# Three joint units at each norm: x times scale first, inverse root and shift on their PSUM banks

## Chip, core and metric

The kernel runs on one core of one Trainium2 chip. The metric is the device time of one execution in microseconds; the time before is the median of three runs. PE is TensorE, DVE is VectorE, ACT is ScalarE, POOL is GpSimd, SP is the queue that issues the weight loads.

## What is computed

A trunk of two layers over 128 context tokens and 256 latent tokens, D = 1024, all in fp32. What matters here is where the norms stand:

```
h   = rmsnorm(x) * (1 + scale1) + shift1
u, q, k, v, z, xbc, dt = split(h @ w_in)            # three mixers, gates, merge
x   = x + gate1 * (merged @ w_out)
h2  = rmsnorm(x) * (1 + scale2) + shift2
up  = dwconv3(h2 @ ffn_w_up)
x   = x + gate2 * ((silu(up_a) * up_b) @ ffn_w_down)
```

`rmsnorm` divides each token by the root of its mean square over D (plus 1e-6). Scale, shift and gate are vectors of D for each of the two token groups, the six parts of `silu(c) @ w_mod + b_mod`.

## The kernel before

Activations lie transposed: 128 channels on the partitions, eight tiles of channels, and 386 columns for the tokens: 256 latent ones, a gap of two columns (`LAT:CTX0`), 128 context ones. The gap is zero; the three-tap convolutions read across it. Every product is made of three matmuls (`three`, lines 787 to 789): a value is cut into a high half that TensorE takes without loss and a low half, and high x high, low x high, high x low are summed in one PSUM bank. ScalarE makes the high halves (line 1102 for weights, 1119 for activations), VectorE the low ones (1423 and 1428).

The work of a layer is a list of units, one weight tile of 128x1024 each: 8 XBC, 4 UU, 4 QQ, 4 KK, 4 VV, 4 ZZ, 24 GATE, 12 BRANCH, 8 OUT, 44 UP, 24 DOWN (three for each of 8 output tiles). Every engine walks that list in order in a program of its own and waits on semaphores of the others; so an instruction that waits holds all behind it on its engine. Four PSUM banks are used in turn by the groups, and a unit may open its bank when the group four before has been read (`group_read`). Three weight tiles are held as halves, four as raw data: when unit u is done, ScalarE makes the high half of unit u+3 and VectorE the low half (`ahead`, lines 1121 and 1430), which TensorE waits for (`wait_lo`).

After a unit of XBC or UP, ScalarE evacuates the bank with the centre tap (`evac`, 1199), VectorE adds the outer taps (`taps`, 1549 and 1551), ScalarE makes a tanh (1237) and VectorE a product (1558, 1562 or 1568); a pair of UP groups then gives a tile `ah`, `al` for DOWN.

An OUT or DOWN group is added into x by VectorE (`update`, 1606, two pieces, latent and context), ScalarE squares the tile (1181) and GpSimd sums the squares (605). At a norm TensorE multiplies that sum by a matrix of ones (`mean_squares`, 739), ScalarE makes the inverse root `rs` (1112, 1113), and then tile by tile VectorE makes x times rs (1443), ScalarE scale and shift (1141, two pieces) and the high half (1119), VectorE the low half (1428). The three first units behind a norm are joint: for each tile of h their three products are made together, so that they follow the norm tile by tile (`joint`, 852). There are four norms with joint units: N1 and N2 of layers 0 and 1, and a last one without units.

The scale, shift and gate vectors are made by VectorE as well, from streamed tiles of `w_mod`: one tile after a unit given by `mod_places` (126), two multiply-and-sum passes of 128x1024 (`modulation`, line 1477), against rows of silu(c). Layer 0 has such tiles after 16 units UU to VV, after 8 units in the mixers, after every third UP unit from UP2 on (14), and after the first 22 DOWN units; layer 1 after the 12 units before ZZ and after every fifth UP unit from UP4 on (8). The rows are loaded anew for the FFN and turned into silu by ScalarE (`row_tanh`, 1171) and VectorE (`rows_silu`, 1463) right behind the second norm.

Of the kernel before, what the change touches and what calls it, by code (L numbers as in the profile page):

```python
# [30 lines left out]
P = 128  # L31
# [52 lines left out]
DOWN0 = U_OF[(DOWN, 0, 0)]  # L84
PREP = DOWN0 + MOD_HEAD + 2
MIX0 = U_OF[(ZZ, 0, 0)]
UU0, BRANCH0, OUT0 = U_OF[(UU, 0, 0)], U_OF[(BRANCH, 0, 0)], U_OF[(OUT, 0, 0)]
# [38 lines left out]
def mod_places():  # L126

    tiles = [(l, m) for l in range(DEPTH) for m in range(MODT)][MOD_HEAD:]
# [78 lines left out]
def scan_task(s, lag=0):  # L207

    y_, rest = divmod(s - lag - SLOT_Y, Y_SLOTS)
    return y_ if rest == 0 and 0 <= y_ < NY else None  # L210


# [59 lines left out]
def build(nc, wstream, whead, par, bias, tab, xs, xp, cvec, cvec_rows, kc, vc, st0, fng, y, newk, newv, news):  # L272
    ctx = ExitStack()
    with ctx:
# [99 lines left out]
        fg = sb("fg", [P, KT])  # L374
        bm = sb("bm", [P, NBIAS])

        acc_all = ctx.enter_context(nc.psum_tensor("acc", [P, BANKS, 512], F32))
# [60 lines left out]
        sq_sum = sem("sq_sum")  # L438
        rs_ready = sem("rs_ready")
        h_full = sem("h_full")  # L440
        h_hi = sem("h_hi")
# [291 lines left out]
        def _(pe):  # L733
# [57 lines left out]
            def unit(l, u):  # L791
# [47 lines left out]
                else:  # L839
                    g = G_OF[(kind, j)]  # L840
                    bank = open_bank(g)
                    first = SP_MG if (kind, j) == (OUT, 0) else None
                    srch, srcl = (mh, ml) if kind == OUT else (hh, hl)
# [7 lines left out]

            def joint(l, u0, split0):

                kind = UNITS[u0][0]
                banks = []
                if l == 0 and u0 == 0:
                    pe.wait_ge(crow_ready, 2)
                for i in range(JOINT):
                    wait_lo(pe, l * NU + u0 + i)
                    g = G_OF[(kind, i)]  # L860
                    if g >= BANKS:
                        group_read(pe, l, g - BANKS)
                    banks.append(acc[g % BANKS])

                def product(i, k):
                    s = (l * NU + u0 + i) % NHL
                    return three(banks[i][:, 0:T], wh[:, s, P * k:P * k + P], wl[:, s, P * k:P * k + P], hh[:, k, :],
                                 hl[:, k, :], k == 0, k == KT - 1)

                for k in range(KT - 2):  # L870
                    if l == 0 and u0 == 0 and k in (2, 4):
                        shift_pair(k // 2 + 1)
                        shift_sums(k // 2 + 1)

                    pe.wait_ge(h_lo, count(l, NSPLIT, split0 + k))
                    for i in range(JOINT):
                        product(i, k)
                pe.wait_ge(h_lo, count(l, NSPLIT, split0 + KT - 1))
                for i in range(JOINT):
                    product(i, KT - 2)  # L880
                    product(i, KT - 1).then_inc(unit_used, 1)

# [189 lines left out]
            for l in range(DEPTH):  # L1072
                if l:
                    mean_squares(l, 0, 2 * l)
                for u in range(NU):
                    if u in (0, UP0):
                        if u:
                            mean_squares(l, M_N2, 2 * l + 1)
                        joint(l, u, SP_N2 if u else SP_N1)
# [10 lines left out]
        def _(act):  # L1090
# [35 lines left out]

            def norm(l, nth, split0, scale, shift0):

                for j in range(KT):
                    b = cv[:, j % 2, :]  # L1130

                    act.wait_ge(h_full, count(l, NFULL, (F_N2 if nth else F_N1) + j))

                    if l == 0 and nth == 0:
                        if j % 2 == 0 and 2 <= j <= KT - 4:
                            shift_part(j // 2 + 1)
                        act.wait_ge(scale_ready, j // 2 + 1)
                    else:
                        act.wait_ge(scale_ready, KT // 2 + 2 * l + nth)
                    for v, (a0, a1) in enumerate(SEGS):  # L1140
                        last = af(b[:, a0:a1], b[:, a0:a1], ACT.Identity, bias=mod[:, shift0 + j, v:v + 1],  # L1141
                                  scale=scale[:, j, v:v + 1])
                    step.then(last)
                    high(l, None, hh[:, j, :], b)

# [37 lines left out]
            def evac(l, g):  # L1183
                kind, j = GROUPS[g]
                bank = acc[g % BANKS]
                group_done(act, l, g)
                if kind in (XBC, UP):
                    n = j if kind == XBC else 8 + j
# [159 lines left out]
            for l in range(DEPTH):  # L1348
# [7 lines left out]
                norm(l, 0, SP_N1, sc1, 0)  # L1356
                if l == 0:
                    params(l)

                act.wait_ge(par_ready, l + 1)  # L1360
                for u in range(NU):
                    if u == UP0:
                        inv_rms(l, M_N2, D)
                        norm(l, 1, SP_N2, sc2, 3 * KT)
# [6 lines left out]
                    if u in (0, UP0):  # L1371
                        ahead(l, u)
# [6 lines left out]
                    for g in done:  # L1379
                        kind, j = GROUPS[g]  # L1380
                        if kind in (XBC, UP):
                            conv_silu(l, g)
                            if kind == UP and j % 2:
                                high(l, F_FF + j // 2, ah[:, j // 2, :], cv[:, 1, :])
                        if kind in (OUT, DOWN):
                            first = KT * (2 * l + (kind == DOWN))
                            square(first, j, first + j)
                        if kind == BRANCH and j >= 2 * KT:
                            high(l, F_MG + j - 2 * KT, mh[:, j - 2 * KT, :], cv[:, j % 2, :])
# [23 lines left out]
        def _(dve):  # L1413
# [21 lines left out]

            def norm(l, nth, split0):

                dve.wait_ge(rs_ready, 2 * l + nth + 1)
                for j in range(KT):
                    if j >= 2:  # L1440

                        dve.wait_ge(h_lo, count(l, NSPLIT, split0 + j - 2))
                    tt(cv[:, j % 2, :], x[:, j, :], rs[:, :], ALU.mult).then_inc(h_full, 1)
                    if j:
                        low(l, split0 + j - 1, hl[:, j - 1, :], cv[:, (j - 1) % 2, :], hh[:, j - 1, :])
                low(l, split0 + KT - 1, hl[:, KT - 1, :], cv[:, (KT - 1) % 2, :], hh[:, KT - 1, :])

# [320 lines left out]

            low_merged = []

            dve.wait_ge(cs_in, 32)
# [5 lines left out]
            for l in range(DEPTH):  # L1777
# [19 lines left out]
                else:  # L1797
                    norm(l, 0, SP_N1)
                for u in range(NU):
                    if u == UP0:  # L1800
                        norm(l, 1, SP_N2)
                        rows_silu(l + 2, crow, junk_ffn)
                    if u == PREP and l + 1 < DEPTH:
                        params(l + 1)

                        summed(l + 1, 0, MOD_HEAD)
                        scale_of(sc1, norm1_weight(l + 1), KT).then_inc(scale_ready, 1)
                    if u in (0, UP0):
                        ahead(l, u)
                    done = done_after(u)  # L1810
                    for g in done:
                        if GROUPS[g][0] in (XBC, UP):
                            group_done(dve, l, g)
                            taps(l, g)
                        if GROUPS[g][0] == BRANCH:
                            branch(l, g)
# [5 lines left out]
                    for g in done:  # L1822
# [11 lines left out]
                        if kind in (OUT, DOWN):  # L1834
                            update(l, g)
                    while low_merged:
                        jj = low_merged.pop(0)
# [3 lines left out]
                    if last_update:  # L1841
                        ahead(l, u)
                    if (l, u) == (0, LATE_ROWS):
                        rows_silu(1, crow_late, junk_late)
                    modulation(l, u)
                    if u == MIX0 - 1:

# [137 lines left out]
```

## Time and profile before

| what | value |
|---|---|
| median of 3 runs | 1437.79 us (1434.54 to 1438.02) |
| the profiled execution | 1435.48 us, span 1433.7 us |
| PE busy | 1349.9 us, 94% |
| DVE busy | 1058.4 us, 74% |
| ACT busy | 651.9 us, 45% |
| POOL busy | 155.8 us, 11% |
| mean granted TensorE clock | 0.974 of full speed |
| last chain, by engine | PE 64%, DVE 22%, issue 6%, ACT 6% |

The busy shares are averages over stages. In 650 to 710 us, in the DOWN stage of layer 0, VectorE is busy over 99% while TensorE is too; in the second half of layer 1 VectorE is about half busy. The last chain is followed back from the last instruction, each step to what released it.

### The profile page before, as it was taken

What the parts mean: (1) busy time and instruction counts of PE and PEld (TensorE: products, weight loads), DVE (VectorE), ACT (ScalarE), POOL (GpSimd) and SP (SyncE); (2) the same over time, 40 slices, a digit from 0 to 9 for tenths busy, and PEclk for the clock granted to TensorE, in tenths of its full rate; (3) what the DMA queues carried; (4) which work ended last, traced back from release to release, by engine and by line L of the source; (5) the groups of instructions that cost most, each with busy time, mean ns of one, the idle gap of its engine ahead of it and who ended that gap; (6) DMA issues with size and microseconds to landing.
All of it is one profiled execution on the core that took longest, in us unless ns stands there. A gap on an engine that the chain in (4) does not pass through costs nothing.

```text
span 1433.7 us, 20178 instructions
## 1 busy us (share of the span) xinstructions
PE 1349.9 (94%) x7702; PEld 1296.8 (90%) x7702; DVE 1058.4 (74%) x1853; ACT 651.9 (45%) x1031; POOL 155.8 (11%) x179
## 2 busy tenths in 40 slices
PE   5899999999997999999979999999999799999995
PEld 4798788899997999999969988899999799999995
DVE  5789877578756999999966787626877588888332
ACT  4643444544446444542345335454444654454331
POOL 0066000000310000000111800000021100000001
PEclk8999999999998999999989999999999999999998
DMA  9456434322343455557734562332224244444431
GB/s 364 135 203 216 153 127 160 126 89 89 104 129 105 163 163 175 165 180 249 261 133 132 182 229 74 102 105 89 76 94 131 98 157 153 138 156 129 132 122 44
DMA packets 58289, 208.94 MB, mean 146 GB/s; under 512 B 6737, under 2 KB 8913, under 8 KB 56785
## 3 DMA queue, kind: packets, MB, share of 16 engines
q1 hardware_dynamic: 55648, 197.52, 41.4%
q0 software_dynamic: 2544, 10.14, 2.0%
q8 instruction: 61, 1.00, 0.3%
q14 instruction: 36, 0.29, 0.1%
HBM read 203.95 MB, written 3.68 MB: 145 GB/s over the span
## 4 chain that ended last, share of the span: by engine, by line
PE 64%; DVE 22%; issue 6%; ACT 6%; DMA 1%; POOL 1%; SPq 0%; ACTq 0%; DVEq 0%; POOLq 0%
PE acc L787 19%; PE acc L789 18%; PE acc L788 18%; DVE wl L1423 6%; DVE junk_ffn L1477 4%; PE mix L1020 2%; PE mix L998 2%; DVE cv L1549 2%; DVE cv L1551 2%; DVE junk_front L1477 1%; ACT cv L1141 1%; PE mix L925 1%; DVE gates L1588 1%; DMA head<-in_whead_dram 1%; ACT wh L1102 1%
## 5 line engine op out<-in xcount | busy, mean ns | idle before, releaser
L787 PE MATMUL acc<-hh,wh 128*128 128x386 f32 x1600 | 561.7, 351 | 27.1 <-DVE hl L1428 21.2
L789 PE MATMUL acc<-hh,wl 128*128 128x386 f32 x1600 | 549.4, 343 | 0.0
L788 PE MATMUL acc<-hl,wh 128*128 128x386 f32 x1600 | 548.8, 343 | 0.0
L1423 DVE TENSOR_TENSOR wl<-raw,wh 128x1024 fp32r<-128x1024 f32 (+1 forms) x280 | 344.1, 1230 | 160.9 <-ACT wh L1102 158.8
L1102 ACT ACTIVATE wh<-raw 128x1024 fp32r<-128x1024 f32 (+1 forms) x280 | 291.1, 1041 | 149.6 <-PE acc L789 149.6
L787 PEld LDWEIGHTS acc<-hh,wh 128*128 128x128 f32 x1600 | 306.5, 192 | 38.1 <-issue 22.4
L788 PEld LDWEIGHTS acc<-hl,wh 128*128 128x128 f32 x1600 | 308.4, 193 | 2.7
L789 PEld LDWEIGHTS acc<-hh,wl 128*128 128x128 f32 x1600 | 307.1, 192 | 0.0
L787 PE MATMUL acc<-ah,wh 128*128 128x386 f32 x352 | 119.3, 339 | 0.0
L788 PE MATMUL acc<-al,wh 128*128 128x386 f32 x352 | 119.2, 339 | 0.0
L789 PE MATMUL acc<-ah,wl 128*128 128x386 f32 x352 | 119.1, 338 | 0.0
L1477 DVE SCALAR_TENSOR_TENSOR junk_ffn<-rawm,crow 128x1024 f32<-128x1024 f32 x88 | 108.7, 1273 | 0.0
L1199 ACT ACTIVATE cv<-acc,prm 128x386 f32<-128x386 f32 x104 | 69.0, 663 | 26.5 <-PE acc L789 26.0
L1549 DVE SCALAR_TENSOR_TENSOR cv<-acc,prm,cv 128x385 f32<-128x385 f32 x104 | 64.1, 617 | 21.1 <-ACT cv L1199 18.1
L1119 ACT ACTIVATE ah<-cv 128x386 fp32r<-128x386 f32 x44 | 23.2, 527 | 120.6 <-DVE cv L1568 120.6
L1477 DVE SCALAR_TENSOR_TENSOR junk_front<-rawm,crow 128x1024 f32<-128x1024 f32 x56 | 74.0, 1357 | 0.0
L1225 ACT ACTIVATE gates<-acc,bgh 128x386 f32<-128x386 f32 x48 | 28.0, 583 | 96.3 <-PE acc L789 96.2
L1551 DVE SCALAR_TENSOR_TENSOR cv<-acc,prm,cv 128x385 f32<-128x385 f32 x104 | 64.4, 619 | 3.7
L788 PEld LDWEIGHTS acc<-al,wh 128*128 128x128 f32 x352 | 66.5, 189 | 0.0
L787 PEld LDWEIGHTS acc<-ah,wh 128*128 128x128 f32 x352 | 66.4, 189 | 0.0
L789 PEld LDWEIGHTS acc<-ah,wl 128*128 128x128 f32 x352 | 66.2, 188 | 0.0
L1237 ACT ACTIVATE th<-cv 128x386 f32<-128x386 f32 x60 | 31.8, 531 | 58.1 <-DVE cv L1551 58.1
(233 smaller groups left out, 1591.6 us busy)
## 6 DMA issues: line engine op xcount, KB each, us to landing
raw<-in_wstream_dram SPq DMA_DIRECT2D x248, 512.0 KB, 3.6
rawm<-in_wstream_dram SPq DMA_DIRECT2D x80, 512.0 KB, 3.9
raw<-in_wstream_dram SPq DMA_DIRECT2D x32, 448.0 KB, 3.4
head<-in_whead_dram SPq DMA_DIRECT2D x8, 1024.0 KB, 13.9
crow<-in_cvec_rows_dram POOLq DMA_DIRECT2D x2, 1024.0 KB, 7.2
out_y_dram<-gates POOLq DMA_DIRECT2D x8, 193.0 KB, 2.7
prm<-in_par_dram POOLq DMA_DIRECT2D x2, 591.5 KB, 4.9
x<-in_xs_dram SPq DMA_DIRECT2D x1, 1024.0 KB, 8.3
```

Source lines behind the costliest of these rows:

```text
L787: mm(out, sh, mhi, start=start, stop=False)
L788: mm(out, sh, mlo, start=False, stop=False)
L789: return mm(out, sl, mhi, start=False, stop=stop)
L998: last = mm(bank[:, P * i:P * i + P], adt[:, col:col + 1].to_broadcast([P, P]), tri[d], start=True, stop=True)
L1020: last = mm(out, s_, m_, start=(n == 0), stop=(n == len(terms) - 1))
L1102: af(wh[:, s, 0:n], raw[:, raw_slot(u), 0:n], ACT.Copy).then_inc(hi_done, 1)
L1199: af(cv[:, b_, :], bank[:, 0:T], ACT.Identity, bias=prm_(b, tile), scale=prm_(w, 3 * tile + 1)) \
L1237: af(th[:, b_, :], cv[:, b_, :], ACT.Tanh).then_inc(cv_tanh, 1)
L1423: tt(wl[:, s, 0:n], raw[:, raw_slot(u), 0:n], wh[:, s, 0:n].bitcast(F32), ALU.subtract).then_inc(lo_done, 1)
L1477: last = stt(out=junk[:, v, :], in0=rawm[:, n % NMOD, :], scalar=1.0, in1=rows[:, v, :], op0=ALU.mult, op1=ALU.mult, accum_out=macc[:, m, ...
L1549: step.then(stt(out=b[:, 1:T], in0=bank[:, 0:T - 1], scalar=prm_(w, 3 * tile), in1=b[:, 1:T], op0=ALU.mult, op1=ALU.add))
L1551: stt(out=b[:, 0:T - 1], in0=bank[:, 1:T], scalar=prm_(w, 3 * tile + 2), in1=b[:, 0:T - 1], op0=ALU.mult, op1=ALU.add).then_inc(cv_done, 1)
```

## The change

N1 of layer 0 is as it was. For the other three norms:

- As each tile of x is updated in OUT or DOWN, ScalarE writes x times scale as the high half (`scaled`, two pieces) and VectorE the low half (`low_scaled`, two pieces), a unit later. The gap columns take the two shift vectors.
- The joint units run on these. Their bank then holds W x (scale x), and in the gap W x shift. The matrix of ones comes after their first step, between their products.
- Meanwhile the norm is made as before, in the places of the scaled tiles, each high half waiting for the joint step that has read the place (`joint_step`). Tiles 6 and 7 wait for the joint units' end; in front of them stand the halves of the fourth unit's weights.
- Before such a group is evacuated, VectorE saves its gap columns, multiplies the bank by rs, adds the gap vector of each token group, and clears the gap (`rescale`).
- The FFN's silu rows are made before the groups of UP3, not before those of UP0. Of the streamed `w_mod` tiles, layer 0's UP ones start at UP4, DOWN keeps 18 of 22, and layer 1 has 16 (UU to VV) instead of 12; for layer 1 the scales come first.

```diff
+STEPS = ((0, 1), (2,), (3,), (4,), (5,), (6, 7))
+EARLY = 6
+ROWS_FFN = UP0 + JOINT
-    units += [(0, UP0 + 3 * i + 2) for i in range(14)] + [(0, DOWN0 + i) for i in range(22)]
-    units += [(1, MIX0 - 12 + i) for i in range(12)] + [(1, UP0 + 5 * i + 4) for i in range(MODT - MOD_G2)]
+    units += [(0, UP0 + 3 * i + 4) for i in range(14)]
+    units += [(0, u) for u in range(DOWN0, NU - 1) if UNITS[u][2] < 2 or u < DOWN0 + 6]
+    units += [(1, u) for u in FRONT] + [(1, UP0 + 5 * i + 4) for i in range(MODT - MOD_G2)]
...
+            def joint(l, nth):
...
+                pe.wait_ge(scaled_lo, shifted_count(l, nth))
+                for n, ks in enumerate(STEPS):
+                    if n == 1:
+
+                        mean_squares(l, M_N2 if nth else 0, 2 * l + nth)
+                    if n == len(STEPS) - 1:
+                        pe.wait_ge(scaled_lo, scaled_count(l, nth, KT - 1))
+                    for i in range(JOINT):
+                        if n == 0:
+                            wait_lo(pe, l * NU + u0 + i)
...
+                        for k in ks:
+                            last = product(i, k)
+                        if n == len(STEPS) - 1:
+                            last.then_inc(unit_used, 1)
+                    if n < len(STEPS) - 1:
+                        last.then_inc(joint_step, 1)
...
+            def norm(l, nth):
+
+                u0 = UP0 if nth else 0
+                for n, ks in enumerate(STEPS):
+                    for j in ks:
+                        affine(l, nth, j)
+                        if n < len(STEPS) - 1:
+
+                            act.wait_ge(joint_step, step_count(l, nth, n))
+                            high(l, None, hh[:, j, :], cv[:, j % 2, :])
+                ahead(l, u0)
+                for j in STEPS[-1]:
+
+                    act.wait_ge(unit_used, count(l, NU, u0 + JOINT - 1))
+                    high(l, None, hh[:, j, :], cv[:, j % 2, :])
+
+            def scaled(l, nth, j):
...
+                if j == EARLY:
...
+                    af(hh[:, :, LAT:CTX0], mod[:, shift0:shift0 + KT, :], ACT.Copy).then_inc(scaled_hi, 1)
+                for v, (a0, a1) in enumerate(SEGS):
+                    last = af(hh[:, j, a0:a1], x[:, j, a0:a1], ACT.Identity, scale=scale[:, j, v:v + 1])
+                last.then_inc(scaled_hi, 1)
...
+            def rescale(l, g):
+
+                bank = acc[g % BANKS]
+                step.then(nc.vector.tensor_copy(wsh[:, :], bank[:, LAT:CTX0]))
+                step.then(tt(bank[:, 0:T], bank[:, 0:T], rs[:, :], ALU.mult))
+                for v, (a0, a1) in enumerate(SEGS):
+                    ts(bank[:, a0:a1], bank[:, a0:a1], wsh[:, v:v + 1], None, ALU.add)
+                nc.vector.memset(bank[:, LAT:CTX0], 0.0).then_inc(rescaled, 1)
...
                     for g in done:
                         if GROUPS[g][0] in (XBC, UP):
                             group_done(dve, l, g)
+                            if joint_group(l, g):
+                                rescale(l, g)
                             taps(l, g)
```

## Rows read from the trace of the kernel before

**Rows 1.** TensorE's waits, whole span: who for whom, us in total, times, longest.
```profile
PE acc L787 <- DVE hl L1428: 21.2, 6, 5.0
```
**Rows 2.** Timeline of TensorE, layer 0's N2: start us, us, instruction, idle before and releaser.
```profile
433.34 0.34 PE L789 MATMUL acc<-mh,wl 128*128 128x386 f32 x1
...
436.96 0.89 PE L739 MATMUL misc<-sqa,tb 128*128 128x386 f32 x2 [3.28 <-POOL sqa L605]
...
458.56 0.45 PE L787 MATMUL acc<-hh,wh 128*128 128x386 f32 x1 [2.01 <-DVE wl L1423]
...
464.44 0.34 PE L787 MATMUL acc<-hh,wh 128*128 128x386 f32 x1
...
481.48 0.34 PE L787 MATMUL acc<-hh,wh 128*128 128x386 f32 x1
```
**Rows 3.** Stretches: length; PE, PEld, DVE, ACT, POOL busy (count); PEclk, DMA share, GB/s.
```profile
460.00:465.00 5.00, 5.00 (x24) 5.00 (x23) 3.96 (x6) 2.93 (x6) 0.00 (x0) 0.74 0.36 112
```
**Rows 4.** Timeline of ScalarE and VectorE, layer 0's N2, the norm.
```profile
437.89 0.58 ACT L1112 ACTIVATE rs<-misc,tb 128x386 f32<-128x386 f32 x1 [2.64 <-PE misc L739]
438.50 0.53 ACT L1113 ACTIVATE rs<-rs 128x386 f32<-128x386 f32 x1
...
439.66 0.98 ACT L1141 ACTIVATE cv<-cv,mod,sc 128x256 f32<-128x256 f32 x2 [0.63 <-DVE cv L1443]
...
451.30 0.56 DVE L1428 TENSOR_TENSOR hl<-cv,hh 128x386 fp32r<-128x386 f32 x1 [0.88 <-ACT hh L1119]
```
**Rows 5.** Timeline behind the last OUT unit of layer 0.
```profile
433.72 0.74 DVE L1606 SCALAR_TENSOR_TENSOR x<-acc,g1h,x 128x256 f32<-128x256 f32 x2 [1.21 <-PE acc L789]
433.78 1.06 ACT L1102 ACTIVATE wh<-raw 128x1024 fp32r<-128x1024 f32 x1 [0.70 <-PE acc L789]
...
434.87 1.22 DVE L1423 TENSOR_TENSOR wl<-raw,wh 128x1024 fp32r<-128x1024 f32 x1 [0.41 <-ACT wh L1102]
435.32 1.49 POOL L605 TENSOR_TENSOR sqa<-sqa,th 128x386 f32<-128x386 f32 x1 [1.17 <-ACT th L1181]
```
**Rows 6.** Timeline of VectorE in layer 0's UP stage: taps UP0, UP3, weights UP8.
```profile
458.42 0.61 DVE L1549 SCALAR_TENSOR_TENSOR cv<-acc,prm,cv 128x385 f32<-128x385 f32 x1
...
470.21 0.62 DVE L1549 SCALAR_TENSOR_TENSOR cv<-acc,prm,cv 128x385 f32<-128x385 f32 x1
...
478.29 1.22 DVE L1423 TENSOR_TENSOR wl<-raw,wh 128x1024 fp32r<-128x1024 f32 x1
```
**Rows 7.** Layer 1: matrix of ones, taps of UP3, weights and start of UP8.
```profile
1126.97 0.56 PE L739 MATMUL misc<-sqa,tb 128*128 128x386 f32 x1 [3.28 <-POOL sqa L605]
...
1157.81 0.61 DVE L1549 SCALAR_TENSOR_TENSOR cv<-acc,prm,cv 128x385 f32<-128x385 f32 x1
...
1168.30 1.21 DVE L1423 TENSOR_TENSOR wl<-raw,wh 128x1024 fp32r<-128x1024 f32 x1
...
1171.53 0.34 PE L787 MATMUL acc<-hh,wh 128*128 128x386 f32 x1
```
**Rows 8.** TensorE at layer 1's N1: last of DOWN, first of units 3 and 5.
```profile
728.23 0.33 PE L789 MATMUL acc<-ah,wl 128*128 128x386 f32 x1
...
755.86 0.45 PE L787 MATMUL acc<-hh,wh 128*128 128x386 f32 x1 [0.35 <-DVE wl L1423]
...
765.04 0.34 PE L787 MATMUL acc<-hh,wh 128*128 128x386 f32 x1
```
**Rows 9.** Groups: engine, operation, shapes, count; busy us, mean ns; idle before.
```profile
L1199 ACT ACTIVATE cv<-acc,prm 128x386 f32<-128x386 f32 x104 | 69.0, 663 | 26.5 <-PE acc L789 26.0
...
L1625 DVE TENSOR_SCALAR pr<-pr,rcp 128x384 f32<-128x384 f32 x16 | 6.7, 421 | 0.6
...
L1728 DVE TENSOR_SCALAR ut<-misc,prm 128x386 f32<-128x386 f32 x8 | 4.9, 615 | 0.3
```
**Rows 10.** The same stretch ahead of the mixers in layers 0 and 1.
```profile
120.00:150.00 30.00, 28.76 (x141) 25.26 (x140) 29.69 (x42) 8.92 (x12) 9.87 (x10) 1.00 0.75 250
...
818.75:848.75 30.00, 30.00 (x149) 26.81 (x148) 28.34 (x45) 10.04 (x13) 3.32 (x4) 1.00 0.83 280
```

More of the change, by code:

```diff
@@ L210, in scan_task, with scaled_count, shifted_count, step_count @@
     return y_ if rest == 0 and 0 <= y_ < NY else None
+def scaled_count(l, nth, j):
+    return (2 * l + nth - 1) * (KT + 1) + j + (j >= EARLY) + 1
+def shifted_count(l, nth):
+    return (2 * l + nth - 1) * (KT + 1) + EARLY + 1
+def step_count(l, nth, i):
+    return (2 * l + nth - 1) * (len(STEPS) - 1) + i + 1
+def joint_group(l, g):
+    kind, j = GROUPS[g]
+    return j < JOINT and (kind == UP or kind == XBC and l > 0)
+def rescaled_count(l, g):
+    kind, j = GROUPS[g]
+    return (2 * l + (kind == UP) - 1) * JOINT + j + 1
+def bank_before(g):
+    return max(i for i in range(NG) if i % BANKS == g % BANKS)
 def count(l, per, i):
@@ L841, in unit @@
                     bank = open_bank(g)
-                    first = SP_MG if (kind, j) == (OUT, 0) else None
+                    first = SP_MG if (kind, j) == (OUT, 0) else SP_N2 if u == UP0 + JOINT else SP_N1 if l and u == JOINT else None
                     srch, srcl = (mh, ml) if kind == OUT else (hh, hl)
@@ L1072, in _ @@
             for l in range(DEPTH):
-                if l:
-                    mean_squares(l, 0, 2 * l)
                 for u in range(NU):
[L1076 to L1079, printed above, removed]
+                    if l == 0 and u == 0:
+                        first_joint()
+                    elif u in (0, UP0):
+                        joint(l, int(u == UP0))
                     elif u not in (1, 2, UP0 + 1, UP0 + 2):
@@ L1125, in ahead, with affine @@
                     hi(n // NU, n % NU)
-            def norm(l, nth, split0, scale, shift0):
-                for j in range(KT):
[L1130 to L1144, printed above, removed]
+            def affine(l, nth, j):
+                scale, shift0 = (sc2, 3 * KT) if nth else (sc1, 0)
+                b = cv[:, j % 2, :]
+                act.wait_ge(h_full, count(l, NFULL, (F_N2 if nth else F_N1) + j))
+                for v, (a0, a1) in enumerate(SEGS):
+                    last = af(b[:, a0:a1], b[:, a0:a1], ACT.Identity, bias=mod[:, shift0 + j, v:v + 1],
+                              scale=scale[:, j, v:v + 1])
+                step.then(last)
@@ new lines, in first_norm @@
+            def first_norm():
+                for j in range(KT):
+                    if j % 2 == 0 and 2 <= j <= KT - 4:
+                        shift_part(j // 2 + 1)
+                    act.wait_ge(scale_ready, j // 2 + 1)
+                    affine(0, 0, j)
+                    high(0, None, hh[:, j, :], cv[:, j % 2, :])
+            def norm(l, nth):
[10 more added lines that the diff above has]
+                    high(l, None, hh[:, j, :], cv[:, j % 2, :])
@@ L1355, in _ @@
                         hi(l, u)
-                norm(l, 0, SP_N1, sc1, 0)
-                if l == 0:
+                    first_norm()
                     params(l)
+                else:
+                    norm(l, 0)
                 act.wait_ge(par_ready, l + 1)
@@ L1370, in _ @@
                         act.preload_act_table_set(LN_EXP)
-                    if u in (0, UP0):
+                    if l == 0 and u == 0:
                         ahead(l, u)
@@ L1387, in _ @@
                             square(first, j, first + j)
+                            if kind == OUT:
+                                scaled(l, 1, j)
+                            elif l + 1 < DEPTH:
+                                scaled(l + 1, 0, j)
                         if kind == BRANCH and j >= 2 * KT:
@@ L1434, in ahead, with norm @@
                     lo(n // NU, n % NU)
-            def norm(l, nth, split0):
+            def norm(l, nth):
+                u0, split0 = (UP0, SP_N2) if nth else (0, SP_N1)
                 dve.wait_ge(rs_ready, 2 * l + nth + 1)
@@ L1769, in _ @@
             low_merged = []
+            pending = []
             dve.wait_ge(cs_in, 32)
@@ L1804, in _ @@
                         params(l + 1)
-                        summed(l + 1, 0, MOD_HEAD)
-                        scale_of(sc1, norm1_weight(l + 1), KT).then_inc(scale_ready, 1)
-                    if u in (0, UP0):
+                        at = MODT * (l + 1)
+                        stt(out=mod[:, 0:KT, :], in0=macc[:, 0:KT, :], scalar=0.5,
+                            in1=bm[:, at:at + KT].unsqueeze(2).to_broadcast([P, KT, 2]), op0=ALU.mult, op1=ALU.add) \
+                            .then_inc(shift_ready, 1)
+                    if l == 0 and u == 0:
                         ahead(l, u)
+                    while pending:
+                        low_scaled(*pending.pop(0))
                     done = done_after(u)
@@ L1835, in _ @@
                             update(l, g)
+                            if kind == OUT or l + 1 < DEPTH:
+                                pending.append((l, 1, j) if kind == OUT else (l + 1, 0, j))
                     while low_merged:
@@ L1842, in _ @@
                         ahead(l, u)
+                        while pending:
+                            low_scaled(*pending.pop(0))
                     if (l, u) == (0, LATE_ROWS):
```

77 lines of the change are left out of this document (56 added, 21 removed).

## The prediction

> **What bounds the kernel now.** I read the page first: TensorE is busy 94% of the span, VectorE 74%, and the chain that ended last runs mostly through the matmuls of the units. So only idle TensorE time, or matmuls at the lower clock, can be won. The list of TensorE's waits comes next: its largest line is the wait of the first product for the first low half of the normed activations, 21.2 us in all [rows 1]. It stands at the norms. Then the timeline of TensorE at the second norm of layer 0 [rows 2]: the last OUT product ends at 433.68 (call that t0), TensorE idles 3.28 us until the mean-square matmul, idles again for the norm, ends the three joint units at 456.55 (t0+22.9) and idles 2.01 us before unit UP3 at t0+24.9. UP4 starts at t0+30.8: UP3 took 5.88 us, where a unit at full clock takes 4.26 (UP4 at 464.44 to UP8 at 481.48, four units in 17.04). In 460 to 465 us the granted clock is 0.74, a mix of the two levels 1.2 and 2.4 GHz [rows 3]. Every long idle is thus paid twice, about 1.6 us on top for slow matmuls.
>
> The joint stage needs 72 matmuls of 0.177 us, 12.7 us, and the matrix of ones about 0.8 us. The stretch from t0 to UP3 lasts 24.9 us, so at most 11.4 us are to be had there, the same in layer 1, and some 13.8 us at the first norm of layer 1 (728.56 to 755.86 [rows 8]): 36.6 us. The question is what VectorE and ScalarE do behind the joint units, and there the answer is against the change.
>
> **The upper bound on VectorE in the UP stage.** After the norm VectorE works through the groups in its own order: taps of group u, low half of the weights of unit u+3, then the rest. TensorE starts UP8 when UP7 is done at 481.48; the low half of UP8 was ready at 479.51 [rows 2, 6]. So VectorE is ahead by only 2.0 us. In layer 1 the same two are 1171.53 and 1169.51, again 2.0 us [rows 7]. A delay of VectorE beyond that reaches TensorE, and as TensorE is full afterwards it is never won back.
>
> **The joint stage after the change (times from t0).** The scaled splits add to each OUT unit two ScalarE pieces of the kind of the affine pair (0.98) and two VectorE pieces of the kind of the update pair (0.74) [rows 4, 5]. Both fit a unit of 4.24 us: ScalarE 1.06 for high weights, 0.53 for the square (as the second root piece, of the same size) and 0.98, VectorE 1.23+0.74+0.74. TensorE's joint start waits only for six pairs and the gap columns, ready at t0 within 0.2. What is late next is the third unit. VectorE must first finish the low half of tile 6 (ScalarE's part of it ends at about 0.8), update tile 7 until 2.3, and then split the weights of UP2 (1.22), until 3.4; before, the update began at 0.04 and that split ended at 2.4 [rows 5]. TensorE wants it at 2.1 and idles 1.3. The squares of tile 7 go through POOL (1.49) until about 4.4, when TensorE's first step ends, so the matrix of ones hardly waits. It ends at 5.3, the root (0.58+0.53) at 6.4, and the joint units at about 14.9 instead of 22.9.
>
> Then the norm itself. From the first root instruction to the last low half it took 437.89 to 451.86, 14.0 us [rows 4]. ScalarE, with two affine pieces and a high half a tile, sets that pace also now, since the steps of the joint units are done sooner than it comes to their tiles. Root starts at 5.3, plus 14.0 is 19.3; into it are put the high and the low half of UP3's weights (1.06 and 1.22), which gives 21.4 for VectorE's last low half and 20.2 for UP3's weights. TensorE, done at 14.9, idles 5.3 us and starts UP3 at 20.2, at the lower clock, until 26.1. So far 4.7 us are won.
>
> **The PSUM repair.** Each joint group now costs VectorE, ahead of its evacuation: a copy of two columns (0.2), a multiplication of 386 columns in PSUM (0.6, as the taps, 0.61 [rows 6]), two additions of 256 and 128 columns (0.7, as the update pair 0.74), a memset (0.1): 1.6 us. No row of before shows these on these operands; the ends are 1.0 (half of the pair's price for the additions, small ones overlapped) and 2.1 (every piece drained at 0.15 more). A tensor-scalar of 386 columns out of PSUM takes 615 ns, one of 384 in SBUF 421 [rows 9], and I take the PSUM price. ScalarE's evacuation (663 ns [rows 9]) was done beforehand for the first group and came while VectorE was at other work for the rest; now it lies between repair and taps with VectorE waiting: 0.7 more. So 2.3 us a group, 6.9 a norm.
>
> The Trainium skill (VectorE: DVE Perf Modes, "Why PSUM operands drop a tier") says that any PSUM operand takes fp32 work to one element a cycle. The two rows just quoted agree. Were it not so, the repair of a group would be 0.2 us cheaper, 0.6 a norm; by the rule it is as in my sum.
>
> **VectorE's chain, N2.** Before: taps of UP0 at t0+24.7, of UP3 at t0+36.5 with one modulation tile (2.4) between them [rows 6], so 9.4 us for three groups without it; in layer 1, where no tile lies there, taps of UP3 at t0+34.1 (t0 is 1123.69) [rows 7]. After: 21.4, repair 2.3, then 9.4 + 2 x 2.3, then the conditioning rows that have moved here: product, tanh that ScalarE can begin only with the second product's input, product, 1.22+1.06+1.22 and hand-overs, 3.6 with VectorE waiting. Taps of UP3 at 41.3: 7.2 later than before at an equal number of tiles. On the way UP4's weights come at 30.9 (before, UP4 began at 30.8) and UP5's at 37.2 (35.0): the lead is gone, TensorE idles 4.8 us before UP4 and falls to the lower clock. UP6's weights come at 41.3+1.25+1.15 = 43.7; after that idle UP6 takes 5.9, UP7 4.3, and UP8 starts at 53.8 instead of 47.8; by VectorE alone it would be 45.8+7.2 = 53.0. **Cost 6.0 us in each layer, 12.0.** The first tile moves from UP2 to UP4, which leaves one tile before UP8's weights either way.
>
> **N1 of layer 1.** VectorE loses 4 of 22 tiles in DOWN and gets eight low halves; it is no longer behind there, but TensorE was full, so nothing is won inside DOWN. At its end the tile of the last but one unit (2.4) still lies before the last update, which ends at about 2.2, the third unit's weights at 3.4. The norm runs as above: last low half 21.2, unit 3 at 20.2. Then repair 23.5, taps 24.8, tanh and product 26.0, repair 28.3, taps 29.5, weights of unit 4 at 30.7 (32.1 before); at the lower clock until 36.5. Unit 5 started at 765.04, which is 36.5 after 728.56 [rows 8]. **Nothing won.**
>
> **Moved tiles.** Layer 1 gets 16 instead of 12 tiles ahead of the mixers, as layer 0 has. Over the same stretch of the stage, 30 us, layer 0 shows 141 matmuls and layer 1 149, with VectorE full in both [rows 10]: 8 x 0.177 = **1.4 us**. Ends: 0, if the attention stage absorbs it, and 2.5.
>
> Sum: 12.0 + 0 + 1.4 = 13.4 us on the profiled execution's 1435.48 (span 1433.7), 1448.9. The median of the runs is 2.3 above that execution: **1451 us**.
>
> **Rivals.**
> 1. Faster: the repair is nearly free and the evacuation hides behind it. What decides is whether taps of UP3 come before t0+35.5; that asks for 0.4 us a group in place of 2.3. For it speaks that TensorE's own part is 8 us shorter; against it that the pieces hang on each other. Then UP8 starts 0.5 to 1 us earlier at each N2, N1 gives 6, tiles cost 1.4: some 6 us below, 1432. With VectorE wholly out of the way the slow restart of UP3 would remain: 26.1+4x4.26 = 43.1 against 47.8, twice, 6.1 at N1: 1424. Chance 0.13.
> 2. No measurable change: the repair costs 1.0 and half of the evacuation hides, 1.3 a group. N2 is then 3.0 later each, N1 2.5 earlier, tiles 0 to 1.4: +4, 1442. What speaks for it is that neighbours on VectorE overlap by 0.08 us. Chance 0.12.
> 3. The OUT stage becomes a ring: high weights, low weights, update, square, scaled pair and the next high weights wait for each other, 1.06+1.22+0.74+0.53+0.98 less the overlaps of about 0.05 at each, 4.3 us against units of 4.24. If it is 4.55 instead, it lags by 0.3 a unit, TensorE's joint start waits 1.5 and everything behind moves by 1.7 at each N2: 1455. Chance 0.13.
>
> The forecast itself has 0.62, with 1446 to 1456 as its own range. What a measurement here can tell from no change is 0.3%, 4.3 us. Faster 0.13, same 0.12, slower 0.75. The range of 1440 to 1460 takes in rivals 2 and 3 and both ends of the repair (1.0 to 2.1), and leaves out the faster case.
>
> **What would show it.** Joint units end near t0+15 and UP3 starts near t0+20; TensorE waits of 4 to 5 us for low weights before UP3 and UP4 at all three norms; the repair at 1.6 us a group with a VectorE wait of 0.7 for the evacuation; taps of UP3 near t0+41; UP8 near t0+54. If UP8 starts before t0+47 in both layers, the forecast is wrong, and its error lies in the 2.3 us a group or in the 21.4.

## The result

The changed kernel takes 1452.62 us (median of four runs, 1451.55 to 1453.48), the kernel before 1436.89 in the runs beside it: ratio 1.0113, 95% interval 1.0100 to 1.0126. It is slower by 16 us; 1451 was forecast. The profiled execution took 1452.38 us, span 1450.3.

### The profile after

First TensorE's waits, whole span: who for whom, us in total, times, longest.

```profile
PE acc L831 <- DVE wl L1527: 38.5, 16, 5.6
PE acc L831 <- DVE hl L1532: 7.8, 3, 5.0
```

The wait for the first normed tiles, 21.2 us [rows 1], is down to 7.8, which belongs to the norm that was not changed. In its place stands a wait for the low halves of weights, 38.5 us, where it was 7.1 before. The low halves are VectorE's, so TensorE now waits mostly for VectorE's turn. Only the longest wait, 5.63 us once a norm, is still the norm's: it is for the weights of UP3, whose high half ScalarE makes behind its last pieces of the norm (below).

The timeline of TensorE at layer 0's second norm, with the last OUT product ending at 433.35 (t0); the columns are start, length, instruction, idle before it.

```profile
433.92 0.44 PE L831 MATMUL acc<-hh,wh 128*128 128x386 f32 x1 [0.56 <-DVE hl L1560]
...
453.55 0.69 PE L831 MATMUL acc<-hh,wh 128*128 128x386 f32 x1 [5.63 <-DVE wl L1527]
...
463.85 0.50 PE L831 MATMUL acc<-hh,wh 128*128 128x386 f32 x1 [4.14 <-DVE wl L1527]
...
476.57 0.45 PE L831 MATMUL acc<-hh,wh 128*128 128x386 f32 x1 [1.90 <-DVE wl L1527]
...
486.71 0.34 PE L831 MATMUL acc<-hh,wh 128*128 128x386 f32 x1
```

Against [rows 2]: the joint units start 0.6 us after t0 and end at t0+14.6 instead of 22.9. UP3 starts at t0+20.2 instead of 24.9, UP4 at 30.5 (30.8), UP6 at 43.2 (39.3), UP8 at 53.4 (47.8). So 8.3 us are won at the end of the joint units, 4.7 are left at UP3 and 0.3 at UP4, and at UP8 5.6 are lost. In the 35 units behind UP8 that loss stays within 0.3 us.

VectorE and ScalarE at the same place show why. The first two lines are ScalarE's: the last affine piece, then the high half of UP3's weights.

```profile
450.17 0.98 ACT L1199 ACTIVATE cv<-cv,mod,sc 128x256 f32<-128x256 f32 x2 [0.41 <-DVE cv L1548]
451.18 1.06 ACT L1167 ACTIVATE wh<-raw 128x1024 fp32r<-128x1024 f32 x1
...
452.27 1.23 DVE L1527 TENSOR_TENSOR wl<-raw,wh 128x1024 fp32r<-128x1024 f32 x1 [2.20 <-ACT wh L1167]
453.41 1.03 DVE L1532 TENSOR_TENSOR hl<-cv,hh 128x386 fp32r<-128x386 f32 x2
454.35 0.15 DVE L1571 COPY wsh<-acc 128x2 f32<-128x2 f32 x1
454.54 0.57 DVE L1572 TENSOR_TENSOR acc<-acc,rs 128x386 f32<-128x386 f32 x1
455.14 0.75 DVE L1574 TENSOR_SCALAR acc<-acc,wsh 128x256 f32<-128x256 f32 x2
455.84 0.06 DVE L1575 MEMSET acc<- 128x2 f32 x1
...
456.70 0.62 DVE L1678 SCALAR_TENSOR_TENSOR cv<-acc,prm,cv 128x385 f32<-128x385 f32 x1 [0.79 <-ACT cv L1297]
...
474.11 0.62 DVE L1678 SCALAR_TENSOR_TENSOR cv<-acc,prm,cv 128x385 f32<-128x385 f32 x1
```

VectorE's lines begin with the low half of the fourth unit's weights and of the last two tiles. Then come the repair (the rescaling of the bank) in 1.55 us, an idle of 0.79 for the evacuation, and the taps of UP0 at t0+23.4. Two more groups go the same way. The taps of UP3, the last row, start at t0+40.8; before they stood at 36.5 with a modulation tile in front of them, 34.1 without one [rows 6, 7].

At layer 1's first norm (last DOWN product at 733.51, t1) TensorE's rows answer to [rows 8]:

```profile
737.98 0.45 PE L831 MATMUL acc<-hh,wh 128*128 128x386 f32 x1 [2.37 <-DVE wl L1527]
...
755.18 0.69 PE L831 MATMUL acc<-hh,wh 128*128 128x386 f32 x1 [5.63 <-DVE wl L1527]
...
765.57 0.69 PE L831 MATMUL acc<-hh,wh 128*128 128x386 f32 x1 [3.23 <-DVE wl L1527]
...
772.50 0.34 PE L831 MATMUL acc<-hh,wh 128*128 128x386 f32 x1
```

The third joint unit starts after an idle of 2.37, unit 3 at t1+21.7 (27.3 before), unit 4 at 32.1 (32.1), unit 5 at 39.0 (36.5). Units 3 and 4 take 7.15 and 6.93 us, both at a granted clock of 0.59; before they took 4.5 and 4.4.

Ahead of layer 1's mixers, the stretch that answers to [rows 10], start of the UU groups plus the same 36.5 us:

```profile
826.21:856.21 30.00, 28.79 (x141) 25.30 (x140) 29.69 (x42) 8.96 (x12) 9.85 (x10) 1.00 0.75 252
```

141 matmuls, as in layer 0, where layer 1 had 149.

The sum of the stretches below grows by 16.8 us (the first evacuation of a kind is ScalarE's first read of such a bank):

| stretch | before | after | difference |
|---|---|---|---|
| start to OUT end, layer 0 | 433.68 | 433.35 | -0.3 |
| OUT end to DOWN end, layer 0 (N2) | 294.88 | 300.16 | +5.3 |
| DOWN end to first UU evacuation (N1) | 53.72 | 56.23 | +2.5 |
| first UU to first VV evacuation | 63.58 | 65.03 | +1.5 |
| first VV to first GATE evacuation | 36.23 | 37.77 | +1.5 |
| first GATE evacuation to OUT end, layer 1 | 241.60 | 243.21 | +1.6 |
| OUT end to DOWN end, layer 1 (N2) | 294.64 | 299.42 | +4.8 |

The fifth and sixth line are no work of the change. Ten microseconds of the fifth, from 30 us behind the first VV evacuation, first before, then after:

```profile
875.86:885.86 10.00, 10.00 (x49) 9.02 (x49) 8.09 (x22) 4.32 (x13) 0.00 (x0) 0.84 0.15 52
```
```profile
884.77:894.77 10.00, 10.00 (x43) 9.02 (x43) 6.57 (x19) 3.27 (x9) 0.00 (x0) 0.70 0.17 53
```

TensorE is busy throughout in both and gets through 49 and 43 matmuls, at a granted clock of 0.84 and 0.70, mixes of 1.2 and 2.4 GHz in other shares. The experiments below have the VV to GATE stretch at 34.7, 36.2 or 37.8 and the one behind it at 241.6, 243.2 or 244.3, whether they keep the change or not. So these 3.1 us are put down to the single execution and not to the change; no kernel has two traces that would show the spread directly.

### The profile page after: what moved, and what is told of

It is laid out like the page before. It is cut to its first block, busy times and chain, and to the rows that moved or that the text cites. A ratio compares the mean times of both kernels' runs of the same rounds, so it can differ in the third digit from the quotient of the medians.

```text
span 1450.3 us, 20318 instructions
## 1 busy us (share of the span) xinstructions
PE 1360.3 (94%) x7702; PEld 1305.0 (90%) x7702; DVE 1095.0 (76%) x1950; ACT 668.1 (46%) x1082; POOL 160.4 (11%) x179
## 4 chain that ended last, share of the span: by engine, by line
PE 52%; DVE 31%; ACT 9%; issue 7%; DMA 1%; POOL 0%; SPq 0%; ACTq 0%; DVEq 0%
PE acc L831 15%; PE acc L833 14%; PE acc L832 14%; DVE wl L1527 8%; DVE junk_ffn L1606 5%; DVE junk_front L1606 3%; DVE cv L1678 2%; DVE cv L1680 2%; ACT wh L1167 2%; PE mix L1087 2%; PE mix L1065 2%; ACT cv L1199 1%; DVE x L1735 1%; PE mix L992 1%; DVE cv L1697 1%
## 5 line engine op out<-in xcount | busy, mean ns | idle before, releaser
L1606 DVE SCALAR_TENSOR_TENSOR junk_ffn<-rawm,crow 128x1024 f32<-128x1024 f32 x80 | 95.5, 1232 | 0.0
L1606 DVE SCALAR_TENSOR_TENSOR junk_front<-rawm,crow 128x1024 f32<-128x1024 f32 x64 | 85.5, 1371 | 0.0
L1184 ACT ACTIVATE ah<-cv 128x386 fp32r<-128x386 f32 x44 | 23.2, 527 | 123.0 <-DVE cv L1697 123.0
L1276 ACT ACTIVATE th<-x 128x386 f32<-128x386 f32 x32 | 16.9, 528 | 86.1 <-DVE x L1735 86.1
```

Source lines behind the costliest of these rows:

```text
L1606: last = stt(out=junk[:, v, :], in0=rawm[:, n % NMOD, :], scalar=1.0, in1=rows[:, v, :], op0=ALU.mult, op1=ALU.mult, accum_out=macc[:, m, ...
```

## The experiments

The names below: A is the forecast's theory, that VectorE's chain ahead of UP8 (of unit 5 at N1) decides.

**No repair.**

```diff
-                step.then(nc.vector.tensor_copy(wsh[:, :], bank[:, LAT:CTX0]))
-                step.then(tt(bank[:, 0:T], bank[:, 0:T], rs[:, :], ALU.mult))
-                for v, (a0, a1) in enumerate(SEGS):
-                    ts(bank[:, a0:a1], bank[:, a0:a1], wsh[:, v:v + 1], None, ALU.add)
```

> The changed kernel without the bank's copy, multiplication and two additions at the nine joint groups; the memset and its signal stay, so the bank is evacuated as it is (that part of the computation is left out). Theory A (VectorE's chain in front of UP8 and of XBC unit 5 decides): each norm's chain is 3 x 1.55 = 4.6 us shorter, the evacuation's wait stays; UP8 starts near t0+48 instead of 53.4 and 52.5, unit 5 of N1 near 34 instead of 39.0; the time falls by 13 to 15 us to 1438 to 1440. Rival B (the slower part comes from TensorE's idles and slow restarts around UP3, and from the moved tiles, not from VectorE's work per group): the 5.6 us idle before UP3 is untouched, and the time falls by less than 5 us, to 1448 or more.

1437.92 us, ratio to before 1.0009 (0.9997 to 1.0021): 14.7 us below the changed kernel. TensorE's starts of UP4 and UP8 in layer 0 (t0 433.08):

```profile
460.76 0.45 PE L831 MATMUL acc<-hh,wh 128*128 128x386 f32 x1 [1.35 <-DVE wl L1527]
...
481.39 0.45 PE L831 MATMUL acc<-hh,wh 128*128 128x386 f32 x1 [0.52 <-DVE wl L1527]
```

UP4 starts at t0+27.7 and UP8 at 48.3 in both layers; unit 5 of N1 is at 35.4, later than the 34 expected. The idle before UP3 is 5.6 us as with the repair, and the time is that of the kernel before: rival B falls. Even with the repair for nothing, the change wins nothing. What uses up the gain of the early joint units is not measured here in parts; the evacuation wait of 0.79 a group stays in this kernel, and so do the silu rows' 3.6 us ahead of UP3's taps.

**More repair.**

```diff
+                    last = ts(bank[:, a0:a1], bank[:, a0:a1], wsh[:, v:v + 1], None, ALU.add)
+                step.then(last)
+                step.then(tt(bank[:, 0:T], bank[:, 0:T], rs[:, :], ALU.mult))
+                for v, (a0, a1) in enumerate(SEGS):
...
```

> The changed kernel with one more multiplication by the inverse root and one more pair of additions at each joint group (the result of these groups is not the reference's). That adds 0.6 + 0.75 = 1.4 us to each of nine repairs. Theory A: 4.1 to 4.2 us later at each of three norms, 12 to 13 us in all, 1465. Rival B: a part of it hides in VectorE's waits, under 6 us in all, below 1459.

1462.71 us, ratio 1.0178 (1.0162 to 1.0194): 10.1 more than the changed kernel, for 12.6 us of added work, above B's 6 and below A's 12 to 13. UP8 stands at t0+57.5 in layer 0 (53.4) and 56.7 in layer 1 (52.5), 4.2 and 4.1 later, as A has it; N1's unit 5 at 42.3 (39.0) is 3.3 later. These three add up to 11.6 us, 1.5 more than the medians show; that rest stays open.

**The moved tiles alone,** in the kernel before.

```diff
-    tiles = [(l, m) for l in range(DEPTH) for m in range(MODT)][MOD_HEAD:]
+    scales, shifts = range(KT, 2 * KT), range(KT)
+    tiles = [(0, m) for m in range(MOD_HEAD, MODT)] + [(1, m) for m in (*scales, *shifts, *range(MOD_HEAD, MODT))]
...
-    units += [(0, UP0 + 3 * i + 2) for i in range(14)] + [(0, DOWN0 + i) for i in range(22)]
-    units += [(1, MIX0 - 12 + i) for i in range(12)] + [(1, UP0 + 5 * i + 4) for i in range(MODT - MOD_G2)]
+    units += [(0, UP0 + 3 * i + 2) for i in range(14)]
+    units += [(0, u) for u in range(DOWN0, NU - 1) if UNITS[u][2] < 2 or u < DOWN0 + 6]
+    units += [(1, u) for u in FRONT] + [(1, UP0 + 5 * i + 4) for i in range(MODT - MOD_G2)]
```

> The kernel before with the changed kernel's places of the streamed modulation tiles in DOWN of layer 0 and ahead of layer 1's mixers, nothing else (UP keeps its places). Theory A: from the first UU evacuation to the first VV one 1.4 to 1.5 us more in layer 1, VectorE less behind at the end of DOWN, which gives up to 1 us back at N1; 1437 to 1439. Rival C (the moved tiles cost the 4.6 us that the changed kernel shows from XBC to the end of OUT of layer 1): 1441 or more.

1436.41 us, ratio 0.9994 (0.9983 to 1.0006), no difference. UU to VV takes 65.0 us, as in the changed kernel, so the 1.45 us are the tiles'. They are paid back at N1: unit 5 starts at t1+34.1 instead of 36.5, VectorE being less behind at the end of DOWN. Rival C falls.

**The silu rows later,** in the kernel before.

```diff
+ROWS_FFN = UP0 + JOINT
...
-    units += [(0, UP0 + 3 * i + 2) for i in range(14)] + [(0, DOWN0 + i) for i in range(22)]
+    units += [(0, UP0 + 3 * i + 4) for i in range(14)] + [(0, DOWN0 + i) for i in range(22)]
...
+                    if u == ROWS_FFN:
                         row_tanh(l + 2, crow, junk_ffn)
...
                         norm(l, 1, SP_N2)
+                    if u == ROWS_FFN:
                         rows_silu(l + 2, crow, junk_ffn)
```

> The kernel before with the FFN's silu rows made before the groups of UP3 and layer 0's UP tiles from UP4 on, as in the changed kernel, nothing else. Theory A: TensorE starts UP3 about 1.8 us earlier and without the idle of 2.0 us, also UP4 and UP5 are 2.8 us earlier, but the rows then stand in VectorE's chain and cost 3.6 us there, and UP8 starts where it did, near t0+47.8; the time stays within 1 us of before. Rival D (idle time of TensorE and the slow matmuls behind it are what counts): 3.4 us won at each of the two FFN norms, 1430.

1442.05 us, ratio 1.0035 (1.0023 to 1.0047): slower by 4.7, where A had no change and D a gain. In layer 1 (t0 1127.82) UP3 starts at 23.2 and UP5 at 32.4, 1.7 and 2.7 us early as said, and then:

```profile
1166.36 0.45 PE L788 MATMUL acc<-hh,wh 128*128 128x386 f32 x1 [1.76 <-DVE wl L1425]
...
1176.51 0.34 PE L788 MATMUL acc<-hh,wh 128*128 128x386 f32 x1
```
```profile
1166.00:1172.00 6.00, 5.64 (x23) 5.64 (x24) 5.30 (x10) 4.08 (x6) 0.00 (x0) 0.72 0.33 102
```

UP6 waits 1.76 us for VectorE, which has been at the rows, and the granted clock behind that idle is 0.72: UP6 takes 5.9 us for 4.26. UP8 is at 48.7 against 47.8, in layer 0 at 49.9. Moving VectorE's work from in front of UP3 to behind it moves the idle and the slow unit with it, at about the same price (before: 2.0 to 2.2 us in front of UP3, which took 5.9), and short waits are added on the way. D is refuted; A had left out the slow unit behind the moved idle. These delays of 0.9 and 2.1 us are not the whole 4.7: layer 0's DOWN stage is 1.6 us longer than before. There the edit has moved the last streamed tile of the UP stage from UP41 to UP43, right ahead of DOWN's own tiles. That this is the cause is not shown.

**The same repair in another order.**

```diff
+                g0 = G_OF[(UP if nth else XBC, 0)]
+                rescale(l, g0)
                 ahead(l, u0)
                 for j in STEPS[-1]:
                     low(l, split0 + j, hl[:, j, :], cv[:, j % 2, :], hh[:, j, :])
+                rescale(l, g0 + 1)
...
+                group_done(dve, l, g)
...
-                            if joint_group(l, g):
-                                rescale(l, g)
                             taps(l, g)
+                            if joint_group(l, g) and GROUPS[g][1] == 0:
+                                rescale(l, g + 2)
```

> The changed kernel with the same work in another order on VectorE: group 0 is repaired in VectorE's wait for the high half of the fourth unit's weights, group 1 ahead of the taps of group 0, group 2 behind them, so that ScalarE's evacuations run beside repairs. Theory A: the repair's 1.6 us are paid twice a norm instead of three times and the evacuation's wait of 0.8 us never; UP4 starts near t0+28.0 instead of 30.5, unit 5 of N1 near 34 to 35 instead of 39.0, UP8 2 to 4 us earlier than 53.4 and 52.5; 1452.6 falls by 9 to 12 us to 1441 to 1444. Rival E (it is the amount of VectorE's work alone that counts, wherever it stands): no more than 3 us.

1439.49 us, ratio 1.0012 (1.0004 to 1.0021): 13.1 us below the changed kernel with the same instructions, a little more than expected. VectorE in layer 0:

```profile
449.66 0.15 DVE L1575 COPY wsh<-acc 128x2 f32<-128x2 f32 x1
...
451.94 1.23 DVE L1527 TENSOR_TENSOR wl<-raw,wh 128x1024 fp32r<-128x1024 f32 x1 [0.73 <-ACT wh L1167]
453.08 1.03 DVE L1532 TENSOR_TENSOR hl<-cv,hh 128x386 fp32r<-128x386 f32 x2
454.03 0.15 DVE L1575 COPY wsh<-acc 128x2 f32<-128x2 f32 x1
...
454.82 0.75 DVE L1578 TENSOR_SCALAR acc<-acc,wsh 128x256 f32<-128x256 f32 x2
455.49 0.61 DVE L1682 SCALAR_TENSOR_TENSOR cv<-acc,prm,cv 128x385 f32<-128x385 f32 x1
```

The first repair stands in the wait of 2.20 us, of which 0.73 are left; the taps at 455.49 follow the second repair at once, the idle of 0.79 is gone. UP4 starts at t0+28.0 and UP8 at 47.9 in both layers, unit 5 of N1 at 35.4. Rival E falls: the order costs 13 of the 15.7 us.

**Rows kept, with the early repairs.**

```diff
+            pool.wait_ge(crow_ready, 2)
+            pool.dma_start(rows_kept, crow[:, :, :]).then_inc(rows_out, 16)
...
-                        pool.dma_start(crow[:, :, :], cvec_rows).then_inc(crow_in, 16)
+                        pool.dma_start(crow[:, :, :], rows_kept).then_inc(crow_in, 16)
...
+                    if n == len(STEPS) - 1:
+                        ahead(l, u0)
...
-                ahead(l, u0)
...
-                        row_tanh(l + 2, crow, junk_ffn)
...
-                        row_tanh(1, crow_late, junk_late)
...
                 ahead(l, u0)
+                rescale(l, g0)
...
-                        rows_silu(l + 2, crow, junk_ffn)
+                        dve.wait_ge(crow_in, 16 * (l + 2))
```

> As e5, and the silu rows are written to memory once at the start and read back ready made, so that ScalarE's tanh passes and VectorE's products for them are gone (also those in layer 0's mixers), and the fourth unit's weight halves come ahead of the norm's tiles 6 and 7. Theory A: 3.6 us of VectorE's chain at each N2 are gone too, taps of UP3 near t0+33, UP3 near t0+18, UP8 0 to 3 us earlier than in the kernel before, 0 to 3 us in layer 0's mixers; 1428 to 1434. If TensorE's starts, not VectorE's chain, decided, the earlier UP3 would show in UP8 by 2 us against e5 without more.

1428.18 us, ratio 0.9928 (0.9910 to 0.9946). Besides the rows, this kernel has the halves of the fourth unit's weights ahead of the norm's tiles 6 and 7; the two are not tested apart. UP3 starts at t0+17.9, UP8 at 45.9 and 44.3 (47.9 in both with early repairs alone), N1's unit 5 at t1+31.8. UP3 is 2.3 us earlier, UP8 2.0 in layer 0 and 3.5 in layer 1. The profiled execution is the fastest of its six, 1420.40 us against 1427.5 to 1429.6, and the 1.5 us between the layers are the clock: UP4 takes 5.9 us in layer 0 and 4.35 in layer 1, behind idles of 3.23 and 3.26. The tenth kernel, the same at the N2s, has UP8 at 45.9 in both layers. So the gain at UP8 is 2.0, which is also what an earlier UP3 alone would give. The waits speak for VectorE's chain: TensorE waits no more behind UP4, where it waited 1.75 us before UP6 with the early repairs alone, and UP4 is only 0.8 us earlier.

More than at the N2s is won in layer 0's mixers, where the rows for the streamed tiles were made as well. TensorE in the kernel before, then in the kernel before with the rows kept (the next experiment):

```profile
231.64 1.62 PE L953 MATMUL mix<-at,vv 128*128 128x128 f32 x6 [3.24 <-ACT pr L1247]
```
```profile
229.52 0.55 PE L944 MATMUL mix<-tb,pr 128*128 128x128 f32 x3 [0.41 <-DVE pr L1628]
```

VectorE no longer makes the attention wait for 3.6 us of rows, and the 3.24 us of idle are gone. From the first VV evacuation to the end of OUT layer 0 takes 278.5 us here, against 283.5 to 285.1 in the eight kernels that make the rows there.

**Rows kept in the kernel before,** and the same with the moved tiles. The edits are the lines on the rows of the diff above, and for the second that of the moved tiles too:

```diff
-                        rows_silu(l + 2, crow, junk_ffn)
+                        dve.wait_ge(crow_in, 16 * (l + 2))
```

> The kernel before with the silu rows written to memory at the start and read back, nothing else. Theory A: UP3 starts near t0+23.1 (the high half of its weights waits for unit UP0) instead of 24.9 and without an idle over 0.5 us, so without slow matmuls behind it; UP8 1.7 to 2.7 us earlier at each N2, 0 to 3 us in layer 0's mixers; 1430 to 1434. Rival D (idle and slow restart only) says 3.4 at each N2, 1430, and UP8 as much earlier as UP4.

> e7 with the moved modulation tiles of e3 (fewer in DOWN, more ahead of layer 1's mixers). From e3's parts: 2.4 us won at N1, 1.45 lost ahead of the mixers; 0 to 1.5 us below e7.

1431.68 us, ratio 0.9960 (0.9944 to 0.9976), and 1425.82, ratio 0.9920 (0.9899 to 0.9941). The first lies where expected, in part by luck. Its profile has UP3 at t0+24.4, not 23.1, as the joint units ended at 24.0 there (granted clock 0.82 over them, against 0.88 before); UP8 is at 47.2 and 46.4, 0.6 and 1.4 earlier and not 1.7 to 2.7. What makes up for it lies in layer 0's mixers: from the first VV evacuation to the end of OUT 279.7 us, 3.8 to 5.4 less than in the kernels that make the rows there, where 0 to 3 were expected. The second gives 5.9 us more than the first, where 0 to 1.5 were expected, and the intervals do not meet. Its six runs fall into two groups, 1421.8 to 1422.4 and 1429.3 to 1429.8, with nothing at the median between them; its profile is of the slower group and 1.3 us below that of the first. What parts the groups stays open. It has the lowest median here, without a piece of the change but the tiles' places; the two with the early repairs and rows kept are equal to it within the intervals.

**The last tile,** in the changed kernel and in that with early repairs and rows kept.

```diff
-    units += [(0, u) for u in range(DOWN0, NU - 1) if UNITS[u][2] < 2 or u < DOWN0 + 6]
+    units += [(0, u) for u in range(DOWN0, NU - 2) if UNITS[u][2] < 2 or u < DOWN0 + 9]
```

> The changed kernel with the last streamed tile of layer 0's DOWN stage taken from behind the last unit but one to behind the third group, the count unchanged. Theory A: at N1 VectorE's last update ends 2.3 us sooner after the last DOWN product, the idle of 2.37 us in front of the third joint unit goes, and with it about 2.4 us of the chain: UP to unit 5 at 36.6 instead of 39.0 after the last DOWN product; nothing at the N2s; 1450.2. Rival F (the 2.5 us lost at N1 against the forecast are the clock's after the idles): unit 5 stays within 0.7 us of 39.0.

> The same edit on e6 (early repairs, rows kept). There N1 shows almost no third-unit idle in the profile (joint units end at 14.8), so theory A gives 0 to 0.5 us: 1427 to 1428; a gain of 2 us would speak for another cause.

On the changed kernel 1451.56 us, ratio 1.0095 (1.0073 to 1.0117), 1.1 below, within the intervals. The expected 2.4 us are not to be seen in the times; only the profile speaks to them (t1 733.22):

```profile
753.39 0.69 PE L831 MATMUL acc<-hh,wh 128*128 128x386 f32 x1 [5.63 <-DVE wl L1527]
...
769.52 0.34 PE L831 MATMUL acc<-hh,wh 128*128 128x386 f32 x1
```

The idle before the third joint unit is down from 2.37 us to 0.46, unit 3 is at t1+20.2, unit 4 at 30.6 and unit 5 at 36.3: what the forecast had for N1. Of the 2.7 us at unit 5, 1.5 are there at units 3 and 4 and belong to the earlier update. The other 1.2 are unit 4 itself, which takes 5.75 us here at a granted clock of 0.73 and 6.93 in the changed kernel at 0.59, with the same work. So rival F falls for the larger part, but not for all of it. On the early repairs with rows kept: 1428.09 us, ratio 0.9922 (0.9902 to 0.9941), no difference, as expected.

## Why the prediction was right

- **The bound.** That VectorE's chain decides, with its lead of only 2.0 us ahead of UP8, and not TensorE's joint stage, is shown by the first, second and fifth experiment: taking 4.65 us a norm from that chain moves UP8 by 5.0 and 4.2, adding 4.2 moves it by 4.2 and 4.1, and reordering it by 5.5 and 4.6, with UP3 at t0+20.2 each time. In the kernel before, VectorE is busy for 161 of the 197 us of layer 1's UP stage and for 36 of the 98 us of its DOWN stage, so "about half busy" hides how little room the UP stage has.
- **Joint stage.** Forecast end 14.9, UP3 20.2, idle 5.3; measured 14.6, 20.2, 5.6. The mean-square matrix hardly waits. TensorE idled 0.6 at the start (forecast 0.2) and hardly before the third unit at the N2s (forecast 1.3): tile 7's update ended at 1.8 and not at 2.3, and the split of UP2's weights at 3.0 and not at 3.4, just as TensorE came to it.
- **Repair.** Forecast 1.6 and 0.7 a group, measured 1.55 and 0.79. The additions ran at the price of the update pair (0.75), so the PSUM price was right. By the Trainium skill (VectorE: DVE Perf Modes, "Why PSUM operands drop a tier") a PSUM operand holds fp32 work to one element a cycle, and the trace agrees: two scalar operations in PSUM cost no less than the two fused ones.
- **VectorE's chain.** Taps of UP3 forecast t0+41.3, measured 40.8; UP8 53.8, measured 53.4 and 52.5. Cost of the two N2s 12.0, measured 10.1 (5.3 and 4.8). In layer 1 UP6 took 4.4 us behind its idle of 1.92, where the forecast had 5.9 and layer 0 shows 5.9; a wait of 0.52 before UP8 took part of that back. In layer 0 0.3 was won back behind UP8.
- **N1.** Forecast nothing won, measured 2.5 lost. One step that failed is "the tile of the last but one unit (2.4) still lies before the last update, which ends at about 2.2": the update ended at 3.3 after the last DOWN product, since VectorE began that tile only 0.1 us after it. That put unit 4 at 32.1 for a forecast of 30.7. The other is unit 4 itself, forecast at 5.8 us and measured at 6.93, at a granted clock of 0.59. The ninth kernel shows the first step: without that tile unit 4 starts at 30.6. That its unit 5 comes out at 36.3 for the 36.5 forecast owes 1.2 us to a higher clock in unit 4.
- **Moved tiles.** Forecast 1.4 ahead of the mixers, measured 1.45 or 1.46 in each kernel that has them. That they also give 2.4 at N1 in the kernel before was missed; in the changed one it is hidden in the sum of N1.
- **The rest.** The sum was 13.4 and the median moved by 15.7; the profiles differ by 16.8, of which 3.1 in layer 1's mixers are put down to the clock and not to the change. So the forecast's total is partly lucky: it was 1.9 too high at the N2s and 2.5 too low at N1. Its rule that every long idle is paid twice, with 1.6 us of slow matmuls, holds behind most idles of these traces but not behind all, as the last section shows.

## What to carry to other kernels

A stall that is filled on one engine is only won if the engine that feeds the following units has lead enough; read that lead (low weights ready against unit start, 2.0 us here) before counting the idle as gain. Work put between a product and its evacuation on the feeding engine costs its own time and the wait for the next engine's piece; here the repair and its place cost 14.7 us against the kernel without it, and 1.6 us when the same pieces stood in waits that were there (the kernel without them keeps the evacuation wait). And look for work that need not be done at all: rows kept in memory gave 5.7 us, the larger part of it in layer 0's mixers, away from the norms that were being looked at, while the rearranged norm gave nothing.

## What the runs showed of the hardware

- An idle of TensorE much shorter than those of the norms can bring the lower clock, but need not. Behind 1.76 us (rows later, layer 1) the granted clock was 0.72 over 6 us, 23 matmuls where 34 fit, and the unit took 5.88 us for 4.26. Behind 1.75 us (early repair, both layers) it was 1.00 and the unit took 4.35. In the changed kernel idles of 1.90 and 1.92 before UP6 gave 5.88 in layer 0 and 4.37 in layer 1; idles of 3.23 and 3.26 before UP4 (early repair with rows kept) gave 5.89 and 4.35. The idle of 0.35 us in [rows 8] was followed by full clock. So an idle of 1.7 to 3.3 us costs either about 0.1 us more or about 1.6, and its length alone does not tell which.
- In layer 1's mixers the same instructions took 34.7, 36.2 or 37.8 us in the twelve profiled executions, in steps of 1.6 us, and where two were compared the granted clock differed (0.84 and 0.70 over 10 us). Differences of that size between two profiles aren't to be explained by an edit.
- On VectorE a repair's pieces of two columns take 0.15 and 0.06 us, and the pair of additions 0.75 us, no less than a fused multiply-add pair with three operands on the same columns (0.74).
